# Column-by-column token order inside a tile, and 368 instead of 384 keys for inner tiles

## What is computed

```
qkv = (x @ w_qkv).reshape(rows, 64, 3, 16, 64)           # rows = 16
c0 = clip(col - 8, 0, 48)                                # first key column of a query's column
col_in = (key_col >= c0) & (key_col < c0 + 16)
for r in rows:
    r0 = clip(r - 4, 0, 8)                               # first of 8 key rows
    s = q[r] . k[r0:r0+8] + rpb[head, row offset, column offset]
    s = where(col_in, s, -inf)
    mix[r] = softmax(s over the 8 x 64 keys) . v[r0:r0+8]
x = layer_norm(alpha * x + mix @ w_o)
hid = square(relu(x @ w_ff1))
ple = sigmoid(x @ w_ple_gate) * (p @ w_ple_proj)
out = layer_norm(alpha * x + hid @ w_ff2 + ple)
```

## Time and profile before

| | |
|---|---|
| time, median of 3 runs (lowest to highest) | 1212.64 us (1211.74 to 1212.88) |
| the profiled execution's own time | 1212.18 us |
| its span | 1210.4 us |
| PE busy | 1198.8 us, 99% |
| PEld busy | 1004.1 us, 83% |
| DVE, ACT, POOL busy | 71%, 51%, 18% |
| granted TensorE clock | 0.999 |

### The profile page before, as it was taken

One profiled execution on the slowest core, in us unless ns is written; L12 is line 12 of the kernel. 1 busy time (PEld: TensorE's weight loads), 2 busy tenths in 40 slices (PEclk: granted clock), 3 DMA queues, 4 the chain that ended last, 5 costly groups with the idle time before them and its releaser, 6 DMA issues.

```text
span 1210.4 us, 17064 instructions
## 1 busy us (share of the span) xinstructions
PE 1198.8 (99%) x5708; PEld 1004.1 (83%) x5708; DVE 860.4 (71%) x1659; ACT 614.6 (51%) x1194; POOL 214.4 (18%) x262
## 2 busy tenths in 40 slices
PE   9999999999999999999999999999999999999997
PEld 7888888888887888888888888888888888888886
DVE  5785666666667668679677777677764565688786
ACT  5654676767767614244444444444454433333571
POOL 1312555555554424100000000000000000000000
PEclk9999999999999999999999999999999999999999
DMA  9669543344444977593555647566579785778533
GB/s 283 179 191 296 141 111 92 77 126 112 110 128 122 293 207 203 179 330 99 201 202 203 228 173 243 184 216 218 181 273 362 278 292 195 278 241 307 182 105 105
DMA packets 172134, 240.46 MB, mean 199 GB/s; under 512 B 12048, under 2 KB 93072, under 8 KB 171664
## 3 DMA queue, kind: packets, MB, share of 16 engines
q1 hardware_dynamic: 170848, 237.14, 59.9%
q0 software_dynamic: 1056, 2.10, 1.0%
q10 hardware_dynamic: 144, 0.13, 0.0%
HBM read 163.17 MB, written 68.87 MB: 192 GB/s over the span
## 4 chain that ended last, share of the span: by engine, by line
PE 94%; DMA 2%; DVE 2%; issue 1%; ACT 1%; SPq 0%; DVEq 0%; ACTq 0%
PE bank L3304 25%; PE bank L3272 25%; PE bank L1719 12%; PE bank L1902 7%; PE bank L3228 6%; PE bank L1753 5%; PE bank L1858 3%; PE bank L1835 3%; PE bank L1819 3%; PE bank L1783 1%; PE bank L1895 1%; DMA ple_embedding<-embedding_place 1%; DMA v_parts<-v_tile_parts 1%; PE bank L331 1%; DMA k_lo_twice<-k_lo_twice 0%
## 5 line engine op out<-in xcount | busy, mean ns | idle before, releaser
L1054 POOL TENSOR_TENSOR probabilities<-probabilities,total_reciprocal 128x384 f32<-128x384 f32 (+1 forms) x128 | 99.0, 774 | 156.6 <-DVE total_reciprocal L1549 156.5
L3272 PE MATMUL bank<-x_combination,weight_parts 128*128 128x512 f32 x504 | 118.5, 389 | 0.0
L1252 ACT ACTIVATE probabilities<-negated_scores,negated_max 128x384 f32<-128x384 f32 (+1 forms) x128 | 75.5, 590 | 82.3 <-DVE negated_max L1543 82.2
L3272 PEld LDWEIGHTS bank<-x_combination,weight_parts 128*128 128x128 f32 x504 | 94.6, 188 | 19.6
L1719 PE MATMUL bank<-act_T_hi,w_qkv_hi 128*128 128x512 f32 x232 | 93.3, 402 | 0.0
L1719 PE MATMUL bank<-act_T_lo,w_qkv_hi 128*128 128x512 f32 x232 | 91.1, 393 | 0.0
L1719 PE MATMUL bank<-act_T_hi,w_qkv_lo 128*128 128x512 f32 x232 | 91.1, 393 | 0.0
L1543 DVE CUSTOM_DVE_ANT_0 negated_scores<-bank,bias_inner 128x384 f32<-128x384 f32 x96 | 53.2, 554 | 47.8 <-issue 47.3
L2630 ACT ACTIVATE hidden_staging<-hidden_staging 128x512 f32<-128x512 f32 x48 | 30.4, 632 | 95.0 <-DVE hidden_staging L2970 95.0
L3272 PE MATMUL bank<-act_T_hi,weight_parts 128*128 128x512 f32 x240 | 77.3, 389 | 0.0
L3304 PE MATMUL bank<-x_combination,hidden_parts_odd 128*128 128x512 f32 (+1 forms) x324 | 73.1, 381 | 0.0
(11 more groups left out here) (296 smaller groups left out, 2985.1 us busy)
## 6 DMA issues: line engine op xcount, KB each, us to landing
hidden_combinations<-hidden_staging SPq DMA_DIRECT2D x112, 256.0 KB, 2.3
w_ff_in<-in_w_ff SPq DMA_DIRECT2D x27, 1024.0 KB, 8.2
weight_raw<-in_w_ff SPq DMA_DIRECT2D x25, 1024.0 KB, 5.4
weight_raw<-hidden_combinations SPq DMA_DIRECT2D x14, 1024.0 KB, 5.5
hidden_in<-hidden_combinations SPq DMA_DIRECT2D x14, 1024.0 KB, 5.9
v_parts<-v_tile_parts SPq DMA_DIRECT2D x16, 512.0 KB, 7.9
v_hi_lo<-v_parts SPq DMA_DIRECT2D x8, 1024.0 KB, 6.7
weight_raw<-in_na_w_qkv SPq DMA_DIRECT2D x14, 512.0 KB, 3.9
```

The source lines that it names most:

```text
L1054: nc.gpsimd.tensor_tensor(prob[:, u % 4, 0:n], prob[:, u % 4, 0:n], recip[:, u % 4:u % 4 + 1].to_broadcast([P, n]), ALU.mult).then_inc(pro ...
L1252: nc.scalar.activation(prob[:, u % 4, 0:n], score[:, u % 2, 0:n], ACT.Exp, scale=-1.0, bias=nmax[:, u % 4:u % 4 + 1], accum_out=total[:, u ...
L3272: mm = nc.tensor.matmul(bank, w1_part(wp, u, p)[:, k, :], x_part(ap, p, k), start=(k == 0 and n == 0 and p in (1, 5, 6)), stop=(k == KH4 - ...
```

## The change

Inside a tile, token number c * 16 + r now stands for row r and column c: column by column. All views that write or read tokens of a tile are turned accordingly: the destinations of the first stage's copies, the partitions of `bias_in`, the mask (its first 8 rows, each for 16 partitions), the bias tables, and the DRAM views of x, p and out. In this order the last 16 keys of the third tile are its last column, which no query of the middle tile sees. So `keys_of` gives 368 keys (`INNER_KEYS`) for the 6 inner tiles of a head and 256 for the two edge tiles, and scores, bias addition, exponential and normalisation go over so many. The three transposes and the product with v still go over 384; a new DVE memset before the attention loop sets the last 16 columns of the four `prob` buffers to zero.

```diff
+INNER_KEYS = NB - ROWS
+def keys_of(g):
+    return INNER_KEYS if 0 < g < GROUPS - 1 else 2 * P
...
 def token_tile(a, g):
-    return bass.AP(a.tensor, a.offset + g * GC * width, [[GRID_W * width, ROWS], [width, GC], [1, width]])
+    return bass.AP(a.tensor, a.offset + g * GC * width, [[width, GC], [GRID_W * width, ROWS], [1, width]])
...
         def x_dest(part, k, t):
-            return S.act[part][:, k, :].rearrange("p (g r c) -> p r g c", g=GROUPS, r=ROWS)[:, t * 8:t * 8 + 8, :, :]
+            return S.act[part][:, k, :].rearrange("p (g c r) -> p r g c", g=GROUPS, r=ROWS)[:, t * 8:t * 8 + 8, :, :]
...
         def x_raw_dest(k, t):
-            return place.rearrange("p (g r c) -> p r g c", r=ROWS, c=GC)[:, t * 8:t * 8 + 8, :, :]
+            return place.rearrange("p (g c r) -> p r g c", r=ROWS, c=GC)[:, t * 8:t * 8 + 8, :, :]
...
-                    sp.dma_start(bias_in[qr * GC:(qr + 1) * GC, h, r0:r0 + KH, :].rearrange("p r w -> p (r w)"), src)\
+                    sp.dma_start(bias_in[qr:P:ROWS, h, r0:r0 + KH, :].rearrange("p r w -> p (r w)"), src)\
...
-            sp.dma_start(col_mask[:, :], mask).then_inc(S.rpb_stored, 16)
+            sp.dma_start(col_mask[:, :], bass.AP(mask.tensor, mask.offset, [[NB, GC], [0, ROWS], [1, NB]])).then_inc(S.rpb_stored, 16)
...
             def normalise(j, u):
-                n = P * len(blocks_of(u % GROUPS))
+                n = keys_of(u % GROUPS)
...
-                return [src] + [a.rearrange("p (d r c) -> p d r c", d=3, r=ROWS)
-                                for a in (col_mask[:, :], bias_inner[:, h, :], bias_full[:, h, :])]
+                masked = col_mask[:, :].rearrange("p (d r c) -> p d r c", d=3, r=ROWS)
+                return [src, masked] + [a.rearrange("p (d c r) -> p d r c", d=3, r=ROWS)
+                                        for a in (bias_inner[:, h, :], bias_full[:, h, :])]
...
                 for i in range(QUARTER):
                     v_total(3, i)
+            dve.wait_ge(v_sum, 3 * QUARTER)
+            nc.vector.memset(prob[:, :, INNER_KEYS:NB], 0.0)
...
                 for part in range(2):
-                    mm = nc.tensor.matmul(score_ps[u % 2][:, 0:P * len(keys)], q_st[:, par, h, g * P:(g + 1) * P],
-                                          k_st[part][:, par, h, cols], start=(part == 0), stop=(part == 1))
+                    mm = nc.tensor.matmul(score_ps[u % 2][:, 0:n], q_st[:, par, h, g * P:(g + 1) * P],
+                                          k_st[part][:, par, h, first:first + n], start=(part == 0), stop=(part == 1))
```

More of the change, by code:

```diff
@@ L705, in x_raw_dest @@
             place = x_sum42[0][:, k - KC2, :] if k >= KC2 else x_sum3[0][:, k, :]
-            return place.rearrange("p (g r c) -> p r g c", r=ROWS, c=GC)[:, t * 8:t * 8 + 8, :, :]
+            return place.rearrange("p (g c r) -> p r g c", r=ROWS, c=GC)[:, t * 8:t * 8 + 8, :, :]
         def x_sum1_dest(k, t):
-            return x_sum1[0][:, k, :].rearrange("p (g r c) -> p r g c", r=ROWS, c=GC)[:, t * 8:t * 8 + 8, :, :]
+            return x_sum1[0][:, k, :].rearrange("p (g c r) -> p r g c", r=ROWS, c=GC)[:, t * 8:t * 8 + 8, :, :]
         def x_turns(k, t):
@@ L1249, in softmax_exp @@
                 g = u % GROUPS
-                n = P * len(blocks_of(g))
+                n = keys_of(g)
                 act.wait_ge(score_done, UNITS * j + (u + 1 + 2))
@@ L1458, in x_sum_third @@
                 dve.wait_ge(x_raw, x_turns(k - KC2, t))
-                dest = x_sum3[0][:, k - KC2, :].rearrange("p (g r c) -> p r g c", r=ROWS, c=GC)[:, t * 8:t * 8 + 8, :, :]
+                dest = x_sum3[0][:, k - KC2, :].rearrange("p (g c r) -> p r g c", r=ROWS, c=GC)[:, t * 8:t * 8 + 8, :, :]
                 nc.vector.tensor_tensor(dest, dest, x_chunk_T(k, t)[:, :, QUARTER:GROUPS, :], ALU.subtract).then_inc(x3_sum, 1)
@@ L1532, in add_bias @@
                 h, g = u // GROUPS, u % GROUPS
-                n = P * len(blocks_of(g))
-                table = bias_inner[:, h, :]
+                n = keys_of(g)
+                table = bias_inner[:, h, 0:n]
                 if g == 0:
@@ L1824, in scores @@
                 h, g = u // GROUPS, u % GROUPS
-                keys = blocks_of(g)
-                cols = slice((g + keys[0]) * P, (g + keys[-1] + 1) * P)
+                n, first = keys_of(g), (g + blocks_of(g)[0]) * P
                 if u == 0:
@@ L2049, in token_columns @@
 def token_columns(a, g, cols):
-    return bass.AP(a.tensor, a.offset + g * GC * D + cols.start, [[GRID_W * D, ROWS], [D, GC], [1, cols.stop - cols.start]])
+    return bass.AP(a.tensor, a.offset + g * GC * D + cols.start, [[D, GC], [GRID_W * D, ROWS], [1, cols.stop - cols.start]])
 def mlp(nc, S, w_ff1, w_ff2, ln_g, ln_b, w_gate, out):
```

## The result

| | before | changed |
|---|---|---|
| time, median of 6 runs each (lowest to highest) | 1212.56 us (1211.31 to 1214.41) | 1242.63 us (1238.43 to 1245.68) |
| span of the profiled execution | 1210.4 us | 1242.0 us |
| PE busy | 99% | 97% |

The ratio is 1.0239, with a 95% interval of 1.0227 to 1.0252: 2.4% slower, about 30 us. The forecast was 1218.2 us with a range up to 1224.0. It had the direction and missed four fifths of the size.

What follows compares the result with a forecast made beforehand. PE was taken as the bound, bound by columns in attention, with other engines able to pace it in the first 46 us. From 1212.18 us, -1.37 +6.0 +0.9 gave 1217.7, or 1218.2 against the median; range 1211.0 to 1224.0 us.

Steps and rivals of the forecast that it cites:

- The bias loads: Loads of bias into SBUF: as many bytes to 8 partitions as before, listed under small things with no cost.
- the 368 keys: Attention stretch: 192 inner-tile score matmuls each lose 16 columns, 7.1 ns, so 1.37 us comes off the end.
- POOL's table work: mask_bias and copy_bias: hopping writes could add 16 us over 8 pairs, hidden by 156.6 us of POOL waiting; nothing.
- The memset: DVE before attention: shorter than 0.69 us and covered by 4.35 us idle, so no cost; uncovered 0.2 us.
- The first stage: First 46 us: copies hopping in SBUF stall PE, 4 us with DVE alone, 8 with ACT too; 6 us taken.
- the layer norm's row: First-stage copy price: DVE operation of 1274, 2366 and 3137 ns, from which slowdown factor 1.86 was chosen.
- a third for early starts: First stage: about a third of stalls given back as next chunk's first four transposes wait only for the first half.
- rival 1: First-stage hops are free: 1211.3 to 1213.1 us; chance 0.29, including any cost so small it stays under 2.4 us.
- The end: Last output stores: 8 by 16 DRAM rows may use half the DMA engines, 0 to 1.8 us later; 0.9 taken.
- Rival 2: First stage: DVE pays for hops, ACT does not, 4 us, 1216.2 us; one half of the forecast's 0.62 chance.
- rival 3: First stage: worst factor 2.46 on both engines, 17 us, about 1229 us; chance 0.06 with what lies down to 1224.
- Rival 4: Score matmuls gain nothing, a fixed cost taking over at 368 columns: 1.4 us more in every case; no separate chance.

Runs made afterwards that it cites:

- e1: Changed kernel with each bias load writing 8 adjacent partitions again instead of 8 that stand 16 apart: 1220.11 us, ratio 1.0061.
- e2: Kernel before with only its bias loads writing 8 partitions that stand 16 apart: 1231.4 us, ratio 1.0148.
- e5: Kernel before with 368 keys for the inner tiles and the memset, without the new token order: 1211.76 us, ratio 0.9988.
- e3: Kernel before with only the destinations of the first stage's copies turned column by column, hops in SBUF: 1219.08 us, ratio 1.0053.
- e4: Kernel before with only the DRAM views of x, p and out turned from 16 by 8 rows to 8 by 16: 1215.75 us, ratio 1.0028.
- e8: Changed kernel with one bias load a head to 128 partitions, a second mask on POOL, and first-stage hops in the PSUM bank: 1214.91 us, ratio 1.0014.
- e6: Kernel before with first-stage copies column by column, but writing SBUF in runs of 8 and hopping in the PSUM bank: 1213.18 us, ratio 1.0000.
- e7: Changed kernel with each bias load writing 8 partitions that stand 2 apart instead of 16: 1250.52 us, ratio 1.0310.

## Why the prediction was wrong

**The step that failed** is one sentence: "The bias loads move as many bytes to 8 partitions as before." It was true and was costed at nothing: a term of the sum put at 0 without a row for it. What it left out is that these DMAs also have a price on the queue that issues them, and that this price changed with the partitions: 295 ns became 543 ns, 256 times. SP's timeline before (32 loads for 11.57 us right ahead of weights, v and the K copies) shows the exposure, if not the 543 ns: none of the rows read from before has a transfer to partitions that are not adjacent. A bound by estimate, one load at up to twice its time, would have been up to 11.6 us at each place where 32 loads stand ahead of the K copies, and the range should have held it. e1 gives its size here, 22 us; e2 alone, 18 us.

**Right, with its size:** the 368 keys, -1.37 us worked out, -1.28 us measured (e5). POOL's table work: `mask_bias` 1014 to 1026 ns, `copy_bias` 503 to 872 ns, and e1, which has both, shows no step from them. The memset takes 0.11 us, in DVE's idle time.

**The first stage: the size right by luck.** Forecast +6, measured +6.4 (e3). Both engines pay, which the prediction left undecided between 4 and 8 us. But the factors are smaller than the 1.86 taken from the layer norm's row: low part 688 to 1074 ns (1.56), sums 410 to 609 ns (1.49), high copy 601 to 1061 ns (1.77), raw copy 500 to 857 ns (1.71, over both its shapes). With these the prediction's own working gives 1.9 us a chunk in place of 2.7 and, over the chunks, about 6 us of stalls. It then took off a third for early starts, which would leave 4. Measured is about the sum without that third, so a too large price and a discount that does not show cancelled. The path was only partly the one forecast: of PE's idle time in this stage, 2.3 us are products that wait for ACT's high copy and 1.6 us are transposes that wait for DVE's sums, while the prediction counted nearly only the second. A smaller slip: the prediction says that its range leaves out the lower edge of rival 1, but 1211.0 lies under that edge, 1211.3.

On this price the Trainium skill, "Vector Engine (DVE) Microarchitecture Reference", section 5.2, has 1.71 to 2.51 ns a column for a side that hops at every element. Here 1074 ns for 512 columns is 2.10 ns, inside that range, with a read and the write hopping. The prediction's estimate from it, 1.0 to 1.4 us, held the measured 1.07 us, and would have been a better source than the layer norm's row, whose 1274 to 3137 ns are a spread between executions of one form.

**The end: mechanism right, size off.** 0.9 us forecast with a bound of 1.8, measured 2.0 to 2.1 us. The bound was the engines' busy time doubled; the issue of ACT's piece alone grew by 0.57 us, which no term held. The same cause has a second place that was not seen: the loads of p, +1.2 to 1.5 us at the last change of pair (e4, e8). The Trainium skill, "DMA: Bandwidth & Descriptors", "Why a DMA increments its semaphore by 16 and not by 1", has a rule by which such a transfer uses 8 engines and not 16. The rule fits both places; no row shows the engines one by one.

**The rivals.** None of them was the cause of the miss. Rival 1 (free hops) falls by e3, but holds for the bank's side (e6). Rival 2 falls by ACT's 1061 ns, rival 3 by its size: 17 us against 6.4. Rival 4 falls by e5 and the 0.165 us. With e1's edit, that is without the failed step, the kernel takes 1220.1 us, inside the range.

**The sum, as measured.** First stage +6.4, 368 keys -1.3, p +1.2, end +2.0: 8.3 us, and e1 has 8.0 us of span. The bias loads on top: 22 to 23.5 us by the times and by the lag.

## What to carry to other kernels

When the partitions or the shape of a DMA change, ask not only for bytes and landing but for its issue time on the queue, times its count, and read in that queue's timeline what stands behind it: here 250 ns more a load delayed copies that PE needed, and at the first change of pair the place in the queue decided whether it cost 0 or 8 us. If a copy must transpose, put the hops on the PSUM side and keep the SBUF side in runs. A gain of 1 us on the critical engine is worth a change only if each transfer and copy that it re-lays has been given a price.

## What the runs showed of the hardware that was not expected

- Issue of a small load on SP: 295 ns to 8 adjacent partitions, 543 ns to 8 partitions 16 apart, 603 ns 2 apart, and 625 ns in the middle for one load to all 128 partitions (before, changed kernel, e7, e8). So one load of 128 partitions issues in the time of one of 8 that are scattered.
- ACT and DVE read a PSUM bank in hops of 64 elements at full speed (601 and 689 ns), while the same copies with hops of 16 elements in SBUF take 1061 and 1074 ns (e6, changed kernel). POOL's copy to such a place goes from 503 to 872 ns, its addition only from 1014 to 1026 ns (before, changed kernel).
- A stall of PE costs more than itself. In the wait at the first change of pair, with PE idle from 157.7 to 164.6 us, the granted clock fell to 0.50, its lower level of 1.2 GHz, and PE's first matmuls after it ran at that level; rows as the stretches above:

```profile
159.00:163.00 4.00, 0.00 (x0) 0.00 (x0) 0.00 (x0) 0.00 (x0) 0.00 (x0) 0.79 0.48 106
163.00:167.00 4.00, 2.44 (x10) 2.42 (x11) 1.49 (x5) 0.76 (x3) 0.00 (x0) 0.50 0.06 11
```

  PE's lag was 18.0 us at the first score matmul of that pair and 19.6 us a few us later, 1.6 us beyond the wait. The clock also fell at 127.2 us, just behind the waits of the first block, and at 400.3 us, in the wait at the last change of pair. In the kernel before it stood at 1.00 through all of these stretches.
